# Moving the stationary buffers hT and yT_a to a multiple of 64 bytes, and the eight rounded-weight buffers to the end of the memory with 32 bytes between each two

## What is computed

```
def swiglu(x, w_gate, w_up, w_down):
    return (jax.nn.silu(x @ w_gate) * (x @ w_up)) @ w_down
...
    proj = u @ w_in
...
    merged = gate_a * (y_a @ w_branch_moba) + gate_b * (y_b @ w_branch_sb)
    return merged @ w_out
...
    x = first_block(...)
    return second_block(x, ...)
```

## Time and profile before

| What | Value |
|---|---|
| median of 3 runs | 1181.34 us (1181.15 to 1181.63) |
| span of the profiled execution | 1178.8 us |
| TensorE matmul busy | 1161.8 us, 99% of the span |
| VectorE / ScalarE / GpSimd busy | 702.3 / 546.1 / 45.7 us |
| DMA | 206.70 MB, mean 175 GB/s |
| granted TensorE clock | 0.9 or more of 2.4 GHz in all 40 slices |

### The profile page before, as it was taken

The page is one execution under the profiler, slowest core; times in us unless marked ns, Lnnn a source line. Parts: engine busy times, 40 slices in busy tenths (PEclk is TensorE's granted clock), DMA queues, the critical chain, the costliest instruction groups (busy, mean ns, idle before and its releaser), DMA issues.

```text
span 1178.8 us, 14513 instructions
## 1 busy us (share of the span) xinstructions
PE 1161.8 (99%) x5412; PEld 946.8 (80%) x5412; DVE 702.3 (60%) x901; ACT 546.1 (46%) x627; POOL 45.7 (4%) x83
## 2 busy tenths in 40 slices
PE   5999999999999999999999999999999999999998
PEld 4888877878888888888888888887777888888887
DVE  4555554745777765555475555467787677555542
ACT  4444442655446444444264444346444564444440
POOL 3000000000000000000000000020041100000000
PEclk9999999999999999999999999999999999999999
DMA  9755468643543665556545556456333345655540
GB/s 301 233 187 190 178 180 252 214 143 108 160 159 128 197 213 178 190 188 228 179 149 189 178 186 232 146 189 222 108 107 108 107 142 180 210 182 178 182 175 36
DMA packets 142527, 206.70 MB, mean 175 GB/s; under 512 B 9240, under 2 KB 100504, under 8 KB 142480
## 3 DMA queue, kind: packets, MB, share of 16 engines
q1 hardware_dynamic: 139296, 198.01, 49.5%
q0 software_dynamic: 2752, 7.47, 2.7%
q10 hardware_dynamic: 432, 0.59, 0.3%
HBM read 203.42 MB, written 2.62 MB: 175 GB/s over the span
## 4 chain that ended last, share of the span: by engine, by line
PE 98%; DMA 1%; DVE 1%; issue 0%; ACT 0%; SPq 0%; DVEq 0%
PE bank L1352 30%; PE bank L1354 29%; PE bank L1353 29%; PE bank L1424 2%; PE bank L1542 1%; PE bank L1541 1%; PE bank L1374 1%; PE bank L1502 1%; PE bank L1554 1%; DMA raw<-in_ffn_w_gate 1%; PE bank L1582 1%; PE bank L1581 1%; PE bank L1580 0%; PE bank L1534 0%; PE bank L1538 0%; PE bank L1590 0%
## 5 line engine op out<-in xcount | busy, mean ns | idle before, releaser
L927 DVE TENSOR_TENSOR w_lo<-raw,w_hi 128x2048 fp32r<-128x2048 f32 (+1 forms) x187 | 426.7, 2286 | 224.2 <-ACT w_hi L640 223.7
L1352 PE MATMUL bank<-w_hi,xT_hi 128*128 128x512 f32 (+1 forms) x1120 | 446.4, 399 | 5.4 <-DVE w_lo L966 5.4
L1354 PE MATMUL bank<-w_hi,xT_lo 128*128 128x512 f32 (+1 forms) x1120 | 436.4, 390 | 0.0
L1353 PE MATMUL bank<-w_lo,xT_hi 128*128 128x512 f32 (+1 forms) x1120 | 435.5, 389 | 0.0
L640 ACT ACTIVATE w_hi<-raw 128x2048 fp32r<-128x2048 f32 (+1 forms) x187 | 354.6, 1899 | 120.6 <-PE bank L1354 99.0
L1352 PEld LDWEIGHTS bank<-w_hi,xT_hi 128*128 128x128 f32 x1120 | 211.0, 188 | 54.1 <-issue 6.6
L1354 PEld LDWEIGHTS bank<-w_hi,xT_lo 128*128 128x128 f32 x1120 | 210.7, 188 | 44.8
L1353 PEld LDWEIGHTS bank<-w_lo,xT_hi 128*128 128x128 f32 x1120 | 211.2, 189 | 40.1
L1352 PE MATMUL bank<-w_hi,hT_hi 128*128 128x512 f32 x352 | 139.9, 398 | 0.0
L1354 PE MATMUL bank<-w_hi,hT_lo 128*128 128x512 f32 x352 | 139.3, 396 | 0.0
L1353 PE MATMUL bank<-w_lo,hT_hi 128*128 128x512 f32 x352 | 139.2, 396 | 0.0
(11 more groups left out here) (245 smaller groups left out, 706.0 us busy)
## 6 DMA issues: line engine op xcount, KB each, us to landing
raw<-in_ffn_w_gate SPq DMA_DIRECT2D x88, 512.0 KB, 3.8
raw<-in_ffn_w_up SPq DMA_DIRECT2D x88, 512.0 KB, 4.7
raw<-in_ffn_w_down SPq DMA_DIRECT2D x88, 512.0 KB, 4.0
raw<-in_w_in SPq DMA_DIRECT2D x76, 512.0 KB, 4.6
raw<-in_w_out SPq DMA_DIRECT2D x16, 512.0 KB, 4.5
raw<-in_w_branch_moba SPq DMA_DIRECT2D x4, 512.0 KB, 4.4
raw<-in_w_branch_sb SPq DMA_DIRECT2D x4, 512.0 KB, 4.3
raw<-in_w_branch_a SPq DMA_DIRECT2D x4, 512.0 KB, 4.3
```

Source lines behind the costliest of these rows:

```text
L927: dve.tensor_tensor(w_lo[s][:, 0:n], raw[s][:, 0:n], w_hi[s][:, 0:n], ALU.subtract).then_inc(lo_done, 1)
L1352: pe.matmul(dst, st(hi), mhi, start=start, stop=False)
L1353: pe.matmul(dst, st(hi), mlo, start=False, stop=False)
L1354: return pe.matmul(dst, st(lo), mhi, start=False, stop=stop)
```

## The change

`w_hi` and `w_lo` are declared last instead of behind `raw`, with a buffer of 8 float32 (32 bytes) between each two; `small` shrinks by two columns, for which `posf` shares the two columns of `ngt` (the first is used in phase F0, the other in M1).

```diff
         raw = [sb(f"raw{i}", [P, UNIT]) for i in range(SLOTS)]
-        w_hi = [sb(f"w_hi{i}", [P, UNIT], F32R) for i in range(SLOTS)]
-        w_lo = [sb(f"w_lo{i}", [P, UNIT], F32R) for i in range(SLOTS)]
         x = sb("x", [P, TT, DM])
...
-        small = sb("small", [P, 258])
+        small = sb("small", [P, 256])
...
-        posf = cols(2)
+        posf = ngt
         bfor = cols(8)
         guess = [sb("guess", [P, 16], I32), pool_cols[:, 4, :].bitcast(I32)]
+        w_hi, w_lo = [], []
+        for i in range(2 * SLOTS):
+            if i:
+                sb(f"shift{i}", [P, 8])
+            w = sb(f"w_{'hi' if i < SLOTS else 'lo'}{i % SLOTS}", [P, UNIT], F32R)
+            (w_hi if i < SLOTS else w_lo).append(w)
```

## The result

The changed kernel takes 1191.24 us (median; 1190.57 to 1191.52) against 1181.24 us for the kernel before on the same chip: ratio 1.0088, 95% interval 1.0074 to 1.0102. It is 0.9% slower. I had predicted 1173.7 us, with a range up to 1190.0. The slower rival stood at 1188.5.

The account below looks back on a forecast made before the run. TensorE's matmul pace was taken to bound the kernel: -7.7 us for the stationary buffers plus 0 for the odd slots' moving buffers gave 1181.3 to 1173.7 us, own range 1172 to 1176, 8-in-10 range 1170 to 1190 us.

Parts of the forecast that it names:

- The slower rival: Odd slots' matmuls, moving at 32 and stationary at 0, pay 6.67 ns each, +14.9 us: 1188.5 us, chance 0.34.
- What bounds the kernel: Whole kernel: TensorE is busy 99% of the span and 98% of the chain, so each nanosecond of a matmul counts.
- The cause: Matmuls reading hT and yT_a: a stationary start 32 bytes past a multiple of 64 costs 6.67 ns per matmul.
- Part 1: hT and yT_a moved to a multiple of 64: 1,152 matmuls at 6.67 ns less, -7.7 us.
- not into a wait: Down products: the time gained does not become a wait, as VectorE's 224 and ScalarE's 121 us idle show.
- Part 2: Odd slots' moving buffers at 32 past a multiple of 64: 0 us on 2,232 matmuls, bounds +14.9 and -29.8 us.
- The row that I leaned on, `sb_sum`: Two 384-column distances, 175 ns each, both operands taken as at 32: a moving operand there pays no own price.
- The 240 ns of the matmul in front: Matmul before `sb_sum`, w_hi at 0 while tri_r at 32 is loaded: 240 ns, nearer 233.3 than 226.7.
- The bound of +14.9 us: Upper bound for the odd slots' moving buffers: 6.67 ns on 2,232 matmuls.
- The odd slots pay: Offset between moving and stationary operand modulo 64, or either start, counts: odd slots lose 14.9 us, 1188.5 us, chance 0.34.
- The distance helps: Odd slots: 32 bytes between PE's two streams save half of 13.3 ns on 2,232 matmuls, -14.9 us: 1158.8 us, chance 0.08.
- it doesn't do what it says: The 6.67 ns come from something else hT and yT_a share, or odd slots give it back: 1181.3 us, chance 0.13.

Follow-up runs that it names:

- the grid: Only matmuls on the core, 64 groups of 48, stationary and moving starts varied in 32-byte steps: 226.7 ns at distance 0, 228.8 at 64, about 233.3 otherwise.
- the third grid: Only matmuls, 96 groups of 48, stationary starts in 4-byte steps, then narrower operands: no start below 226.7 ns; 384 columns take 173.3 at distance 0, 176.7 at 32.
- part 1 alone: Kernel before, with only hT and yT_a moved to a multiple of 64 bytes and the weight buffers left in place: 1175.6 us, ratio 0.9949.
- part 2 alone: Changed kernel, with 32 bytes in front of hT so that it and yT_a start 32 past a multiple of 64 as before: 1191.02 us, ratio 1.0085.
- part 1 at distance 32: Changed kernel, with 160 bytes in front of the eight weight buffers and none between, all 32 bytes past distance 0: 1197.87 us, ratio 1.0148.
- the three grids: Matmul-only runs over 32-byte starts, over finer starts (48 groups), and over 4-byte stationary starts with narrower operands: 226.7 ns was the quickest at 512 columns.
- with the buffers last: Changed kernel, with one 128-byte buffer in front of the eight weight buffers and none between, all at distance 0: 1174.41 us, ratio 0.9951.

## Why the prediction was wrong, point by point

**What bounds the kernel** was right: TensorE's pace and nothing else. 226.7 against 233.3 ns was read rightly too, and so was that no other engine and no DMA has a part in it: the grid shows both values with nothing else running.

**The cause** was the first step to fail. "What differs is the place of the stationary buffer: xT starts at a multiple of 64 bytes, hT and yT_a 32 bytes past one. I take that as the cause." It is the distance between moving and stationary start modulo 256. The kernel before held both at 128 past a multiple of 256 for xT, and both readings fit its three stretches equally well. My slower rival had the idea of a distance, but modulo 64. By that the even slots are safe, and they were not: slot 0 has w_hi at a distance of 128, and slot 2 has 192.

**Part 1** was right as a term, on its own: the down matmuls go to 226.7 ns, and their mean over the trace from 233.3 to 226.9, 6.4 ns on 1,056 of them or 6.8 us. Of the 7.7 us expected the runs show 5.5 (1181.14 to 1175.6). What is missing is mostly the 1.9 us wait at the seam: I had written that the time goes "not into a wait", from VectorE's idle time over the whole kernel, and hadn't looked at the one seam where a late DMA makes VectorE late. The earlier trace rows had the sign of it: 17.4 us of ScalarE's idle time are put down to w_down's loads, not to the slots. yT_a gained 0.3 us and not 0.6: its mean went from 233.0 to 229.4 ns, and its short blocks stand behind transposes.

**Part 2** is the step that decided: "From this I take 0 us." It costs 10 us alone (ratio 1.0085). On top of part 1, as my sum has it, it costs 16: from 0.9949 to 1.0088 of 1181 us, since it takes away what part 1 gained as well. The row that I leaned on, `sb_sum`, was no case of the new kind: its two operands start at 208,544 and 222,880, both 160 past a multiple of 256, so their distance was 0, the cheap one. It is 384 columns wide besides. There the third grid puts distance 0 at 173.3 and distance 32 at 176.7, and the 175 ns of the earlier trace rows lie between the two. A finer reading wouldn't have helped: at 1 ns the two distances are 174 and 176, and with part 1 alone, at distance 0 as well, 171 and 175. The 240 ns of the matmul in front are 235 at 1 ns, and 227 with part 1 alone, where its own two operands lie as before and only the operands of `sb_sum` have moved. I had named the weakness of the row, two distances in steps of 10 ns, and still put the price at nothing, though the term hung on 2,232 matmuls. The bound of +14.9 us didn't hold on top of part 1, and holds for part 2 alone only by luck: it counted the wrong matmuls. Taken over all 4,464 at 6.67 ns the bound is +29.8 us, and part 1 at distance 32 came to 23.5 of it.

**The rivals.** "The odd slots pay" had the right sign and a near time, 1188.5 us, by the wrong account. "The distance helps" is wrong: none of the pairs of starts tried in the three grids beats distance 0 at 512 columns. For "it doesn't do what it says" I cited the Trainium skill (SBUF — State Buffer, Specifications (TRN2), and Who interferes with whom). Its 16-byte lines would make starts in steps of 32 equal, and its independent ports would leave nothing between TensorE's own two operands. Both are what I drew from the page, which gives no pace of matmuls by start. The grid contradicts both: the measurement decides.

## What to carry to other kernels

Where TensorE is the bound and its float32r matmuls are 512 columns wide, the starts of the moving and the stationary buffer in a partition are worth 3% of their time: keep the two equal modulo 256 bytes, at starts that are a multiple of 32 (tried with slices that themselves step by multiples of 512 bytes). A buffer of two odd columns in front of one operand is enough to lose it, and an allocation order that happens to be right should be written down before buffers are moved for another reason. Before a layout change is priced from one trace, ask which other reading of the addresses fits its rows as well; a kernel of nothing but matmuls over a grid of starts answers it in one run.

## What the runs showed of the hardware that I had not expected

- The pace of a 512-column float32r matmul depends on moving start minus stationary start modulo 256 bytes (starts in steps of 32): 226.7 ns at 0, 228.8 at 64, 232.3 to 234.3 at the others. It holds where the hi and the lo buffers have the same distance. Whole multiples of 256 (256, 512, 768) cost nothing.
- Starts off a multiple of 32 can cost more: 240.0 ns at moving 20 and stationary 0, and 238.0 at 4 and 4, although the distance is 0. They aren't settled by the starts alone: moving 0 and stationary 16 took 226.7 ns in one grid and 233.4 in another.
- What comes before matters as well. The same distances, those of slot 1 in the changed kernel, have two steady paces: 231.1 ns in the 23 units directly behind another unit, 235.5 in 12 of the 13 behind a transpose or another small matmul. At distance 0 no such second pace is seen, in part 1 alone or with the buffers last.
- A stationary operand of 32 columns is not quicker than one of 128: 231.7 against 226.7 ns at distance 0.
- A wait of 10.7 us of TensorE also cost clock: 13.65 us at the 1.2 GHz level, where matmuls of 512 columns start 427 ns apart, before it was back at 2.4.
- One write of 1.5 MB takes 34 to 36 us to land and can hold up the weight loads beside it. By its place alone it cost 10.7 us at the start of M0, 1.9 us in F0 once TensorE was quicker, and no wait of TensorE in the middle of M0.
